# Activation tables named ahead of waits, and four pieces of work in another order, in a three-stage transformer kernel

## The reference, cut to what matters

```python
# first block
h = rms_norm(x, pre_gain); q, k, v, z_a, b, c, u, z_c = split(h @ w_in)
attn = rms_norm(diff_attention(q, k, v)) * 0.8 * silu(z_a)
conv_out = b * conv3(c * u) * silu(z_c)
x = x + rms_norm(concat(attn, conv_out) @ w_out)
x = x + sigmoid(x @ w_ple_gate) * rms_norm(p @ w_ple_proj)
# second block
n = rms_norm(concat(meta, x)); c_q, c_kv, k_pe, gq, gk, gv, ga, gg, gate_a, gate_b = split(n @ w_in_2)
y_a = latent_attention(...)   # 8 heads: per-head norms, rope, softmax(q k^T) v
y_b = gated_linear_attention(...) * silu(gg)   # 4 heads, decays exp(cumsum(log_sigmoid))
h = h + (sigmoid(gate_a) * (y_a @ w_o_mla) + sigmoid(gate_b) * (y_b @ w_o_gla)) @ w_out_2
h = h + peer_ffn(rms_norm(h))  # 16384 experts, top 16 of product keys in 8 heads, gelu
```

## Time and profile before

| | |
|---|---|
| time, median of 3 runs | 2169.21 us (2168.06 to 2170.66) |
| the profiled execution's own time | 2159.97 us |
| its span, first to last instruction | 2158.2 us |
| mean granted TensorE clock | 0.996 of full speed |
| busy: PE, PE weight loads, DVE, ACT, POOL | 2104.9, 1656.5, 1308.2, 922.2, 1029.4 us |
| instructions | 27394 |

### The profile page before, as it was taken

The page is one execution under the profiler, slowest core; times in us unless marked ns, Lnnn a source line. Parts: engine busy times, 40 slices in busy tenths (PEclk is TensorE's granted clock), DMA queues, the critical chain, the costliest instruction groups (busy, mean ns, idle before and its releaser), DMA issues.

```text
span 2158.2 us, 27394 instructions
## 1 busy us (share of the span) xinstructions
PE 2104.9 (98%) x10296; PEld 1656.5 (77%) x10296; DVE 1308.2 (61%) x2244; ACT 922.2 (43%) x1528; POOL 1029.4 (48%) x892
## 2 busy tenths in 40 slices
PE   8999999999999999999999999999999899999999
PEld 6877767657887676887887777888888788888887
DVE  6446257253235674214898977888880666666664
ACT  4223343572234334211324447887884443434341
POOL 6665547121324213777759888999995100000000
PEclk9999999999999999999999999999999999999999
DMA  5322322201111111223215665887788988888884
GB/s 198 106 78 71 109 75 93 91 30 40 68 40 59 59 40 59 98 89 126 96 62 159 217 194 172 270 307 253 287 292 315 330 284 298 287 287 290 294 289 147
DMA packets 98291, 359.32 MB, mean 166 GB/s; under 512 B 8480, under 2 KB 41504, under 8 KB 73328
## 3 DMA queue, kind: packets, MB, share of 16 engines
q1 hardware_dynamic: 98160, 357.56, 47.8%
HBM read 286.09 MB, written 71.30 MB: 166 GB/s over the span
## 4 chain that ended last, share of the span: by engine, by line
PE 81%; DVE 11%; POOL 3%; ACT 2%; issue 1%; DMA 1%; SPq 0%; POOLq 0%; ACTq 0%; DVEq 0%
PE ps L1438 11%; PE ps L1439 11%; PE ps L802 10%; PE ps L803 9%; PE ps L804 9%; PE ps L1386 7%; PE ps L1387 7%; PE ps L1249 2%; PE ps L791 2%; DVE area L2413 2%; DVE area L2410 1%; PE ps L1412 1%; PE ps L1413 1%; PE ps L884 1%; DVE area L2441 1%
## 5 line engine op out<-in xcount | busy, mean ns | idle before, releaser
L2577 POOL CAST wring_parts<-wring 128x512 fp32r<-128x512 f32 x236 | 169.7, 760 | 543.5 <-PE ps L804 426.4
L1386 PE MATMUL ps<-sqbuf_parts,wring_parts 128*128 128x512 f32 x1024 | 411.3, 402 | 7.7 <-POOL wring_parts L2621 7.7
L1387 PE MATMUL ps<-normed_x_parts,wring_parts 128*128 128x512 f32 x1024 | 403.2, 394 | 0.0
L2581 POOL TENSOR_TENSOR wring_parts<-wring,wring_parts 128x512 fp32r<-128x512 f32 x244 | 350.9, 1468 | 6.6 <-ACT wring_parts L1852 1.5
L2621 POOL TENSOR_TENSOR wring_parts<-wring_parts,wring 128x512 fp32r<-128x512 f32 x256 | 327.4, 1307 | 45.3 <-ACT wring_parts L1856 45.3
L1386 PEld LDWEIGHTS ps<-sqbuf_parts,wring_parts 128*128 128x128 f32 x1024 | 193.0, 188 | 53.2 <-POOL wring_parts L2621 7.9
L1387 PEld LDWEIGHTS ps<-normed_x_parts,wring_parts 128*128 128x128 f32 x1024 | 193.0, 188 | 41.6
L802 PE MATMUL ps<-resid_parts,wring_parts 128*128 128x512 f32 (+1 forms) x528 | 201.8, 382 | 6.1 <-DVE normed_x_parts L2010 3.3
L803 PE MATMUL ps<-normed_x_parts,wring_parts 128*128 128x512 f32 (+1 forms) x528 | 197.6, 374 | 0.0
L804 PE MATMUL ps<-resid_parts,wring_parts 128*128 128x512 f32 (+1 forms) x528 | 196.8, 373 | 0.0
L1474 ACT ACTIVATE area<-ps 128x1024 f32<-128x1024 f32 (+6 forms) x89 | 61.6, 696 | 275.1 <-PE ps L804 183.5
(11 more groups left out here) (269 smaller groups left out, 4426.8 us busy)
## 6 DMA issues: line engine op xcount, KB each, us to landing
wring<-in_weights_dram SPq DMA_DIRECT2D x65, 1024.0 KB, 4.8
wring<-in_uT_dram SPq DMA_DIRECT2D x128, 512.0 KB, 4.4
area<-in_vT_dram SPq DMA_DIRECT2D x44, 1024.0 KB, 7.2
hidden_table<-area SPq DMA_DIRECT2D x32, 1024.0 KB, 6.6
gate_table<-area SPq DMA_DIRECT2D x32, 1024.0 KB, 8.3
area<-gate_table SPq DMA_DIRECT2D x32, 1024.0 KB, 9.1
wring<-in_vT_dram SPq DMA_DIRECT2D x20, 1024.0 KB, 7.1
rt<-hidden_table SPq DMA_DIRECT2D x32, 512.0 KB, 4.6
```

The lines of the kernel that those rows point to most:

```text
L1386: pe.matmul(out, first[:, d], h_first[:, k, :], start=(k == 0), stop=False)
L1387: mm = pe.matmul(out, rest[:, d], h_rest[:, k, :], start=False, stop=(k == KD - 1))
L2577: ins = nc.gpsimd.tensor_copy(up[:, d, :], W(name)[:, d, :])
L2581: ins = nc.gpsimd.tensor_tensor(low[:, d, :], W(name)[:, d, :], up[:, d, :], ALU.subtract)
```

## The change

- `preload_act_table` names a table ahead of an activation: ahead of the waits of each `root` (Ln), ahead of Silu, Sigmoid and Gelu copies, back to Exp after Silu, once for each group of `roots`. `decay_terms` names the set `natural_log_exp_and_others`, which serves both its Exp and its Ln and the level exponentials after it, and head by head goes back to Exp's set ahead of the Tanh. The roots of g0 to g3 are done in twos (Ln, Ln, Exp, Exp), and `silu(0)` after all four.
- Values: `mv` 1 and 2 are copied by ACT and not by DVE; `mv` 4 is made by PE after the first two scores, and copied by DVE after the first two maxima.
- `exps_m(u + 2)` comes ahead of the copy of the side job of unit u.
- The split of weight gg1 on POOL waits for level 6 of the last gated head and not for `ta3`.
- The first product with w2: k tiles 0 to 5 of both halves, then 6 and 7 of both.

```diff
-    jobs += [("mv", t) for t in LAST_VALUES]
-    jobs += [("MS", 0), ("MS", 1)]
+    jobs += [("mv", LAST_VALUES[0]), ("MS", 0), ("MS", 1), ("mv", LAST_VALUES[1])]
...
             scores_m(0)
             scores_m(1)
+            tokens(("mv", LAST_VALUES[1]), "ukv1", (LAST_VALUES[1],), ckv, 2, 0, 1024)
...
+            def first_w2():
+                key = ("w2", 0)
+                claim(key)
+                up, low = split_arrived("w20")
+                for ks in (range(6), range(6, KD)):
+                    for a in range(2):
+                        d = slice(a * P, (a + 1) * P)
+                        for k in ks:
+                            if a == 0 and k % 2 == 0:
+                                pe.wait_ge(pair_split, 4 * 3 + k // 2 + 1)
+                            mm = three(...)
+                fills(mm, key)
+            first_w2()
+            for m in range(1, 4):
                 project_parts(("w2", m), MIX_PARTS, 3)
...
+            def root(name, width, eps="eps"):
+                logarithms_next()          # act.preload_act_table(ACT.Ln)
+                root_log(name, width, eps) # the waits and the Ln
+                root_exp(name, width)      # the Exp
...
                     if g == "za":
+                        act.preload_act_table(ACT.Silu)
                         copy_out((g, m), zaT[:, 2 * m:2 * m + 2, :], pair((g, m)), ACT.Silu)
+                        if u + 2 < len(UNITS_A):
+                            exponentials_next()
...
             def roots(names):
+                logarithms_next()
                 for name in names:
...
                 if g:
                     roots(PART_GROUPS[g - 1])
+                if g > ROTATE_AT and g in VALUES_AT:
+                    t = VALUES_AT[g]
+                    copy_out(("mv", t), mv[:, t, :], flat(("mv", t)))
...
+                if u + 2 < len(UNITS_M):
+                    exps_m(u + 2)
                 if u in SIDE_M:
                     key = SIDE_M[u]
...
                         copy_gv(*key[1:])
-                if u + 2 < len(UNITS_M):
-                    exps_m(u + 2)
...
             def decay_terms(h):
+                both_next()                # natural_log_exp_and_others
                 when_filled(act, key)
...
                     if n == 3:
+                        exponentials_next()
                         when_filled(act, ("ta", h))
...
-            root("g0", T)
-            root("g1", T)
+            for n in (0, 2):
+                logarithms_next()
+                for h in (n, n + 1):
+                    root_log(f"g{h}", T, "eps")
+                for h in (n, n + 1):
+                    root_exp(f"g{h}", T)
+            act.preload_act_table(ACT.Silu)
             silu(0)
-            root("g2", T)
-            root("g3", T)
...
             for g, names in enumerate(PART_GROUPS):
-                if g in VALUES_AT:
+                if g == ROTATE_AT:
                     copy_values(VALUES_AT[g])
...
-            copy_values(LAST_VALUES[1])
...
             stats_m(0)
             stats_m(1)
+            copy_values(LAST_VALUES[1])
...
                 if i >= NU:
-                    when_filled(pool, last_job(SPLIT[i - NU]))
+                    when_filled(pool, ("lev", HG - 1, 6) if name == "gg1" else last_job(SPLIT[i - NU]))
```

More of the change, by code:

```diff
@@ L1148, in _ @@
                 sum_part(name)
-            for t in LAST_VALUES:
-                tokens(("mv", t), "ukv1", (t,), ckv, 2, 0, 1024)
+            tokens(("mv", LAST_VALUES[0]), "ukv1", (LAST_VALUES[0],), ckv, 2, 0, 1024)
             def scores_m(u):
@@ L1335, in _ @@
                 project_parts(("ob", m), O_PARTS, 2)
-            for m in range(4):
+            def first_w2():
[8 more added lines that the diff above has]
+                                pe.wait_ge(pair_split, 4 * 3 + k // 2 + 1)
+                            mm = three(pair(key)[:, a, :], (up[:, k, d], low[:, k, d]),
+                                       (MIX_PARTS[0][:, k, :], MIX_PARTS[1][:, k, :]), k == 0, k == KD - 1)
+                fills(mm, key)
+            first_w2()
+            for m in range(1, 4):
                 project_parts(("w2", m), MIX_PARTS, 3)
@@ L1482, in square, with logarithms_next, exponentials_next, both_next @@
                 act.activation(dst, src, ACT.Square).then_inc(squared, 1)
-            def root(name, width, eps="eps"):
+            def logarithms_next():
+                act.preload_act_table(ACT.Ln)
+            def exponentials_next():
+                act.preload_act_table(ACT.Exp)
+            def both_next():
+                act.preload_act_table_set("natural_log_exp_and_others")
+            def root_log(name, width, eps):
                 k = NORM[name]
@@ L1623, in _ @@
             root("ple", T)
+            act.preload_act_table(ACT.Sigmoid)
             for m in range(4):
@@ L1867, in _ @@
             round_u(3)
+            act.preload_act_table(ACT.Gelu)
             def beside(t):
```

7 lines of the change are left out of this document (5 added, 2 removed).

## The result

The changed kernel takes 2150.69 us (median of 4 runs, 2148.36 to 2154.98), the kernel before 2168.64 in the same comparison (4 runs, 2166.30 to 2170.66): a ratio of 0.9922, 95% interval 0.9905 to 0.9939. The forecast was 2158.3 us with a range of 2152 to 2165, so the direction is right and the gain was larger than forecast: 18.0 us against 10.9.

The account below looks back on a forecast made before the run. PE, busy 2104.9 of 2158.2 us, was taken as the bound, leaving about 53 us of idle time to win. Terms summed to 10.9 us, taken from the 2169.2 us median: 2158.3 us, range 2152 to 2165.

Parts of the forecast that it names:

- mix: Norm before latent attention: named table brings Ln and Exp 0.9 us earlier, but DVE waits for a product; 0.2 us won.
- gated head 0: One set for both functions removes the load at 674.67 on the chain to levels 1 and 2; 1.25 us won.
- Rival 2: Half-speed stretch behind the wait at the latent norm goes (2154.7 us) or appears behind another (2161.9); chance 0.17, both signs.
- Heads 2 and 3 of the first block: Named table at 235.22 us brings ACT, DVE and the last split 1.28 us earlier; PE wins 0.4 us.
- Group of qn2 and qn3: Named table at 437.63 us: 0.68 us of idle ACT goes through to PE's 2.1 us wait; 0.7 us won.
- Values: At latent attention's first transposes, mv4's own copy refills the wait mv4 was to fill; 0.3 us lost.
- Exponentials: Latent attention: exponentials ahead of side copies remove seven PE waits, three wide and four narrow; 3.9 us won.
- Split of gg1: POOL's split moved off gated head 3's last levels, so levels 5 and 6 come earlier; 2.7 us won.
- Rival 3: POOL's moved split slows DVE's mask and product for transposed keys; 1.1 us go back, 2159.4 us; within the forecast's 0.55.
- Rival 4: Compiler puts its own load behind each named table; only 4.6 us won, 2164.6 us; chance 0.07.
- Rival 5: ACT waits for DVE's maximum ahead of each side copy, making 24 copies late; slower, 2178.8 us; chance 0.03.
- rival 1: Low ends: the next wait stands close behind each one removed; 5.5 us won, 2163.7 us; chance 0.18.

Follow-up runs that it names:

- e8: The changed kernel with VectorE's copy of the last value tile (mv4) moved behind the first two divisions of latent attention; 2148.34 us beside the changed kernel's 2147.92.
- e2: The kernel before plus three orders only (exponentials ahead of side copies, gg1's split behind level 6, first w2 product in two parts); 2154.52 us, ratio 0.9960.
- e12: The changed kernel with mv4's copy behind the first two divisions and GpSimd splitting eight expert tiles, not seven, between routing heads three and four; 2148.05 us.
- e17: The changed kernel with mv4's copy behind the first two divisions and one GpSimd pause, behind the third routing head's place product; 2147.59 us, ratio 0.9920.
- e18: The changed kernel with only one GpSimd pause, behind the third routing head's place product, until VectorE's sums are made; 2145.70 us, ratio 0.9910.

## Why the prediction was right and wrong

**The step that failed** is "The median is 9.2 us above it; I know no row for that difference and carry the sum over unchanged." The difference did have a cause that the change touches: stretches of TensorE at half speed behind waits near 2 us. The one behind level 6 of head 3 is in six of seven traces that have its wait, and not in the trace the sum was made against; those near 446 and 467 us are in two. The change removed the wait at level 6 and cut the one near 446 us to 0.8, and so the median fell by 3.6 us more than by the waits alone: 1143.8 - 1127.6 = 16.2 against 12.6 (3.0 by means). The sum was carried over from an execution that had nothing of this to lose. The other part of the miss is in the sizes of terms: `mix` and gated head 0 came out 0.65 and 0.9 us larger.

**Rival 2 (the clock)** named the mechanism, 3.6 us for "a stretch", and looked for it at one place, behind the wait at `mix`. There it stayed: 0.91, 0.50, 0.91 in the windows from 370 to 385 us of the changed kernel. No profile here gives the clock in GHz, only its share of full speed: at 0.50 the matmuls of 264 columns start 0.22 us apart (378.66 to 380.42 in the changed kernel), which is 1.2 columns a ns, and 0.12 us apart behind the stretch (381.14 to 381.75); that and the share are all that stands here behind the prediction's 1.2 and 2.4 GHz, which are an estimate. The stretches went at places where the trace of before showed none. With a weight of 0.17, for both signs together, it did not move the forecast. The prediction's own last sign of being wrong, that half-speed stretches come or go, did show.

**Heads 2 and 3 of the first block**, 0.4 forecast: 0.2 (from 0.2 us behind at 228 us to level at 350). **`mix`**, 0.2 forecast: 0.85, near the upper bound; the product came 0.34 us earlier, and more of the half-speed stretch fell on the wait instead of on products. **Group of qn2 and qn3**, 0.7: 1.3 at kn2, since DVE's two scalings also took 3.5 us and not 4.2, the first of them now starting 0.1 us ahead of POOL's subtractions (0.8 us of wait left, not 1.4), and 0.7 given back at the rotation, whose wait grew from 0.4 to 1.1. Net 0.6.

**Values**, -0.3: +0.1. The working was right to the engine and the row: mv4's copy, 489.64 for 1.21 us, stands just ahead of reciprocal and division, and the wait grew from 1.63 to 1.79 us. Moving it won 1.8 to 1.9 us by the traces, 2.6 by the medians of the cut kernels.

**Exponentials**, 3.9: 3.99. All seven waits are gone.

**Gated head 0**, 1.25: 2.16. No wait is left at level 2, where I expected 0.5 us. The load itself is 1.28 us of it and no more: each of the 65 and 60 loads shows 1.28 us, and in the kernel before the load at 674.67 ended at 675.95 and the next activation began at 675.97. Where the rest comes from is in the timeline of DVE: with the load gone, its two long steps of level 1 (670.52, 671.65) ran mostly while POOL was still at its casts (668.89 for 3.20 us), in 1.10 and 0.98 us, and not under POOL's subtractions (from 676.75), in 1.78 and 1.64 (677.34, 679.15) as in the kernel before.

**Split of gg1**, 2.7: 2.8. **First product with w2**, 2.05: 2.13. Rival 3 did not come, though POOL's split (814.58 to 819.99) lies over the keys' mask and product, which took 0.73 and 1.02 us there (815.99, 816.62), not 1.75. Rival 4 is excluded by the count of table loads, 60 for 65, five fewer as forecast. Rival 5 is excluded with the exponentials' term, and rival 1 (5.5 us) with the sum: no new wait stood close behind those removed but the one at the rotation.

The terms measured are 0.2 + 0.85 + 0.6 + 0.1 + 4.0 + 2.2 + 2.8 + 2.1 = 12.8 us where 10.9 was forecast: 1.9 of the miss. The clock ahead of the experts is 3.6 of it (3.0 by means). About 2 us are left of the 7.6, which is inside the interval of the ratio (3.7 us either way); the other comparison of the same two kernels has 14.5 us and not 18.0, less than the terms and the clock together (12.8 + 3.0). That the profiled pair came out at 11.6, close to the 10.9, is luck: terms 1.9 us too small, and 1.7 us of clock lost near 1312 in the changed kernel alone.

That the experts' stage passes a gain on unchanged ("what is won ahead of it moves the rest forward as a whole") held for this change by luck of phase: a gain of 2 us more was given back there in full (`e8`), and `e2` lost 5.8 of its 9.2.

**What stays open.** Why DVE's sum is let in between POOL's instructions at the gated heads (two-operand steps of 1.1 to 1.8 us) and is held for up to 14 us in the experts' stage; how often the long hold comes in the whole kernels, since only profiled executions show it; and what else than the clock makes runs at the same clock differ by 8 us.

## What to carry to other kernels

A profiled execution is one draw. If its time lies far from the median, look whether it is the light or the heavy end (its granted clock against those of the other runs), and price a removed wait with the half-speed stretch that can stand behind it: here 1.7 us behind a wait of 2.1 us, in six traces of seven. Cutting the kernel short behind the changed stages made a wander of 11 us (24 runs) into one of 1 to 4 (5 runs each), and single terms of 3 us could be timed. A gain ahead of a stage that two other engines run in step may be taken back by that stage's phase; its own trace says so, the median of the whole kernel does not.

## What the runs showed of the hardware

- A VectorE sum of two SBUF operands (128x256, 0.42 us where GpSimd was still) stood for up to 14.0 us while GpSimd ran subtractions of 1.3 us back to back. The holds of 11.5 and 14.0 us (`before`, `e2`, `e8`) ended in GpSimd's first gap, those of 6.5 and 9.0 us (`e12`; the changed kernel) 0.3 us into a subtraction that then took 1.5 us, with no gap. The longest lay over eleven subtractions in a row. With GpSimd held back after two of its instructions (`e17`, `e18`), both sums took 1.77 us.
- TensorE went to half speed (a granted share of 0.50; matmuls of 264 columns 0.22 us apart and not 0.12, in the changed kernel near 380 us) behind single idle times of 2.0 to 2.3 us in an otherwise busy stretch in some executions and not in others, 1.7 us lost each time; behind idle times of 0.2 to 0.5 us never, nor behind those of 1.6 to 1.8 us near 466, 491 and 985 us. Behind those of 2.75 to 2.94 us (at `mix`, at the first product of the experts and near 1312) it fell in 42 of 46 cases. These are counts of this kernel's places and no threshold.
- A table load of ScalarE took 1.28 us each of the 65 and 60 times. In the kernel before one stands between an Exp and a Ln (664.75), between a Ln and an Exp (674.67), ahead of Silu (142.95), Sigmoid (308.46) and Gelu (1292.32), and none between the level exponential at 685.27, the Tanh at 691.07 and the exponential at 691.99. With the set `natural_log_exp_and_others` named, none stands between Exp (659.52), Ln (660.20) and the level exponentials (669.07 to 678.08).
